# Two blocks of a mixed model, one core: the filter sums of the long convolution on GpSimd in place of VectorE

## The chip, the cores and the metric

One core of a Trainium2 chip runs the whole program once. The metric is device microseconds (us) of that core, as the median over several executions; each profile is one execution, recorded by the hardware profiler. Engines: PE is TensorE (PEld its weight loads), DVE is VectorE, ACT is ScalarE, POOL is GpSimd, and SP issues the DMAs.

## The reference, cut to what matters

A first block of two layers (pooling and attention, then a long convolution and a Fourier mixer) is followed by a second block of two layers. All is float32, 512 tokens, width 1024. The change concerns the filters of the long convolution only:

```python
h = (hdn @ w3).reshape(L, 2, 2, 768)                 # 2 orders, 2 directions, 768 channels
h = h * decay[:, None, None, :]
h = h / (jnp.sum(jnp.abs(h), axis=(0, 2), keepdims=True) + EPS)
kfull = jnp.concatenate([h[:, :, 0], zero, h[:0:-1, :, 1]], axis=0)
...
zf, kf = jnp.fft.rfft(z, n=2 * L, axis=1), jnp.fft.rfft(kfull, n=2 * L, axis=0)
return jnp.fft.irfft(zf * kf[None], n=2 * L, axis=1)[:, :L]
```

## The kernel before, in words

The program is five streams of instructions, one for each engine, written out by hand. Every instruction adds to a semaphore under a label, and `wait_ge(*when(label))` makes an engine wait for that label. An engine works strictly in the order of its stream. So the order of the work around the change is the order of these lines, and whatever stands behind a wait on an engine waits too.

The long convolution treats 768 channels in two halves of 384 (`G = 384`) and two orders, which makes four filters, n = 0 to 3 (`STEPS`). A filter has 512 lags, in four tiles j = 0 to 3 of 128 lags (partitions) by 384 channels. For a tile:

- TensorE (`filters`, L1610) multiplies the hidden layer with `W3`, one product for each direction, into PSUM.
- ScalarE (`decay`, L566) computes the decay `DEC`.
- VectorE (`filter_tile`, L1071) multiplies PSUM with `DEC` into `HH[0]` and `HH[1]`, the two directions. There is one buffer of each.
- VectorE forms `FSUM` (L1076) and `FDIFF` (L1077), their sum and difference, from which the spectrum's cosine and sine parts are made. In tile 0 it copies one row (L1081).
- ScalarE (`magnitudes`, L574) writes the magnitudes `MAG`, and VectorE adds them into `ABSA` (L1085, L1088 in tile 0).

After a filter's last tile TensorE adds `ABSA` over partitions (`norm_sums`, L1615), VectorE turns the result into the norm's inverse (`filter_norm`, L1095 and L1097), and TensorE transforms `FSUM` and `FDIFF` (`transform("hk", ...)`, L1627), after which VectorE combines even and odd parts (`spectrum`, L1109 to L1113).

Filter 0 is made in between the 18 tiles of a three-tap convolution: VectorE does two products with additions for each (L1161 and L1164, both of whose tensors lie in SBUF) and a one-column copy (L1163), and after tiles 2, 6, 10 and 14 (`FILTER_AT`) it does a filter tile. The filters n+1 = 1 to 3 are made in the loop over the steps n = 0 to 2. There VectorE's order is:

```python
filter_tile(n + 1, 0)
filter_tile(n + 1, 1)
spectrum("hz", n, 0)
filter_tile(n + 1, 2)
filter_tile(n + 1, 3)
filter_norm(n + 1)
products(n, 0)
```

and TensorE's order is `to_tokens(n)`, `filters` 0 and 1, `transform("hz", n, 0)`, `filters` 2 and 3, `norm_sums(n + 1)`, `transform("hz", n, 1)`, two `transform("hk", n + 1, ...)` and `back(n)` (L1647). `products` (L1128 to L1137) multiplies the spectra; `output` (L1146 to L1155) follows `back`.

GpSimd's stream before the change has the pooling mixer early in the program (L828 to L847), and then only clears a few tensors at the start of each layer of the second block (L852 to L855). VectorE's work beside the pooling mixer is the norm and rotation of the heads: L982 and L987 with both tensors in SBUF, L993 and L998 likewise, L995 with one of its operands in PSUM.

Of the kernel before, what the change touches and what calls it, by code (L numbers as in the profile page):

```python
# [56 lines left out]
class Ledger:  # L57
# [15 lines left out]
    def did(self, label, by=1):  # L73
        name = label.split(".")[0]
        if self.engine and name not in self.counts:
            name = f"{name.split('_')[0]}_on_{self.engine}"
        self.counts[name] = self.counts.get(name, 0) + by
        assert label not in self.marks, label
        self.marks[label] = (name, self.counts[name], tuple(k for k, _, _ in self.stack))
        return self.sem(name), by  # L80
# [6 lines left out]
    def when(self, label, back=None):  # L87
        if self.known is None:
            return self.sem("unknown_yet"), 1
        name, value, loops = self.known[0][label]  # L90
        for loop in loops:
            per = self.known[1][loop, name]
            here = [var for k, var, _ in self.stack if k == loop]
            if here:
                value = here[0] * per + (value - (per if back == loop else 0))
            else:
                value = value + (self.known[2][loop] - 1) * per
        return self.sem(name), value
# [19 lines left out]
def program(nc, A, known=None):  # L118
# [3 lines left out]
    add, sub, mul = ALU.add, ALU.subtract, ALU.mult  # L122
# [3 lines left out]
    did, when, sem = led.did, led.when, led.sem  # L126
# [5 lines left out]
    def at(offset, shape, dt=f32, name="t"):  # L132
        made[0] += 1
        return nc.alloc_sbuf_tensor_at(f"{name}_{made[0]}", shape, dt, offset=base + offset)
# [44 lines left out]
    def bank(b, n=S, rows=slice(0, P)):  # L179
        return PS[rows, b * S:b * S + n]  # L180

    def z(n, rows=slice(0, P)):
        return Z[rows, n * S:(n + 1) * S]
# [32 lines left out]
    G = 384  # L216
# [3 lines left out]
    FSUM = at(MOD_AT + 12 * KB, [P, 4, G], name="filter_sum")  # L220
    FDIFF = at(RAW_AT + 8 * KB, [P, 4, G], name="filter_diff")
# [3 lines left out]
    MAG = at(SPLIT_AT + 4 * KB, [P, 2, G], name="filter_mag")  # L225
# [10 lines left out]
    HH = [at(o, [P, G], name="filter") for o in (MOD_AT + 18 * KB, RAW_AT + 14 * KB)]  # L236
    PMY = [at(WIDE_AT + 24 * KB + 2 * KB * c, [P, S], name="hy_y") for c in range(2)]
    ABSA, DEC = SQ[0], SQ[1]
# [67 lines left out]
    STEPS = [(g, o) for g in range(2) for o in range(2)]  # L306
    FILTER_AT = (2, 6, 10, 14)
    SPEC_BANK = {"hk": 0, "hz": 4}
    ITEMS = [(h, i, br) for h in range(4) for i in range(NT) for br in range(3)]
    WIDTH = [31 if br == 2 else P * (i + 1) for _, i, br in ITEMS]  # L310
    GROUP_BANK = (0, 2, 5, 1)
    ROT_BANKS = (6, 1, 6, 1)
# [507 lines left out]
    @block.gpsimd  # L820
    def _(pool):
        led.engine = "gpsimd"
        gp = nc.gpsimd

        pool.wait_ge(taken, EV_IN + PRIME)
        pool.wait_ge(*when("in_tabc.all"))
        for c, t in enumerate((PU, PV_, PW_)):
            gp.memset(t[:, :, :], 0.0).then_inc(*did(f"pool_z.{c}"))  # L828
        pool.wait_ge(*when("pool_z.2"))
        for m in range(2):  # L830
            gp.tensor_copy(PU[:, m, 8:8 + S], z(10 + m)).then_inc(*did(f"pool_u.{m}"))
        pool.wait_ge(*when("pool_u.1"))
        gp.tensor_tensor(PV_[:, :, 0:527], PU[:, :, 0:527], PU[:, :, 1:528], add).then_inc(*did("pool_s.2"))
        pool.wait_ge(*when("pool_s.2"))
        gp.tensor_tensor(PW_[:, :, 0:525], PV_[:, :, 0:525], PV_[:, :, 2:527], add).then_inc(*did("pool_s.4"))
        pool.wait_ge(*when("pool_s.4"))
        gp.tensor_tensor(PV_[:, 1, 0:521], PW_[:, 1, 0:521], PW_[:, 1, 4:525], add).then_inc(*did("pool_s.8"))
        pool.wait_ge(*when("pool_s.8"))
        gp.tensor_tensor(PW_[64:P, 1, 0:513], PV_[64:P, 1, 0:513], PV_[64:P, 1, 8:521], add).then_inc(*did("pool_s.16"))
        pool.wait_ge(*when("pool_s.16"))  # L840
        for g, (w, src) in enumerate(((2, PV_), (4, PW_), (8, PV_), (16, PW_))):
            m, rows = g // 2, slice(64 * (g % 2), 64 * (g % 2) + 64)
            gp.tensor_tensor(Z[rows, (10 + m) * S:(11 + m) * S], src[rows, m, 8 - w // 2:8 - w // 2 + S], INVC[rows, m * S:(m + 1) * S], mul).then_inc(*did(f"pool_m.{g}"))
        for g in range(4):
            m, rows = g // 2, slice(64 * (g % 2), 64 * (g % 2) + 64)
            pool.wait_ge(*when(f"pool_m.{g}"))
            gp.tensor_tensor(Z[rows, (10 + m) * S:(11 + m) * S], Z[rows, (10 + m) * S:(11 + m) * S], PU[rows, m, 8:8 + S], sub).then_inc(*did("pool_d.all" if g == 3 else f"pool_d.{g}"))  # L847
        with led.loop(pool, "layers", LAYERS) as lay:
            pool.wait_ge(taken, lay * PER_LAYER + (T_LAYERS + L_OUT + PRIME))
            pool.sem_inc(passed, 1)  # L850
            for c in range(2):
                gp.memset(K2[c][:, :, :], 0.0).then_inc(*did(f"k_zero.{c}"))  # L852
            gp.memset(KC[:, :, :], 0.0).then_inc(*did("k_zero.all"))
            gp.memset(GS[:, :, :], 0.0).then_inc(*did("gla_zero.0"))
            gp.memset(GA[:, :, :], 0.0).then_inc(*did("gla_zero.1"))  # L855
# [3 lines left out]
    def _(dve):  # L859
        led.engine = "vector"  # L860
        v = nc.vector
# [201 lines left out]
        def filter_tile(n, j):  # L1063

            for d in range(2):
                dve.wait_ge(*when(f"hy_filt.{n}.{2 * j + d}"))
                if d == 0:
                    dve.wait_ge(*when(f"hy_dec.{n}.{j}"))
                if j or n:
                    dve.wait_ge(*when(f"hy_abs.{n if j else n - 1}.{(j - 1) % 4}.1"))  # L1070
                v.tensor_tensor(HH[d][:, :], bank(2 * (j % 2) + d, G), DEC[:, 0:G], mul).then_inc(*did(f"hy_d{d}.{n}.{j}"))  # L1071
            dve.wait_ge(*when(f"hy_d1.{n}.{j}"))
            if n:
                dve.wait_ge(*when(f"hk_mm.{n - 1}.1"))
                dve.wait_ge(*when(f"hy_norm_mm.{n - 1}"))
            v.tensor_tensor(FSUM[:, j, :], HH[0][:, :], HH[1][:, :], add).then_inc(*did(f"hy_sd.{n}.{j}.0"))  # L1076
            v.tensor_tensor(FDIFF[:, j, :], HH[0][:, :], HH[1][:, :], sub).then_inc(*did(f"hy_sd.{n}.{j}.1"))  # L1077
            if j == 0:

                dve.wait_ge(*when(f"hy_sd.{n}.{j}.0"))  # L1080
                v.tensor_copy(FSUM[0:1, 0, :], HH[0][0:1, :]).then_inc(*did(f"hy_lag0.{n}"))  # L1081
            for d in range(2):
                dve.wait_ge(*when(f"hy_mag.{n}.{j}.{d}"))
                if j:
                    v.tensor_tensor(ABSA[:, 0:G], ABSA[:, 0:G], MAG[:, d, :], add).then_inc(*did(f"hy_abs.{n}.{j}.{d}"))  # L1085
                    dve.wait_ge(*when(f"hy_abs.{n}.{j}.{d}"))
            if j == 0:
                v.tensor_tensor(ABSA[:, 0:G], MAG[:, 0, :], MAG[:, 1, :], add).then_inc(*did(f"hy_abs.{n}.{j}.1"))  # L1088

        def filter_norm(n):  # L1090
            inv = HINV[n % 2]
# [66 lines left out]
        for j in range(18):  # L1158
            dve.wait_ge(*when(f"conv_mid.{j}"))
            tap = TAP[j % 3]  # L1160
            v.scalar_tensor_tensor(tap[:, 1:S], z(j + 1)[:, 0:S - 1], col("conv_w", j), tap[:, 1:S], mul, add).then_inc(*did(f"conv1.{j}"))  # L1161
            dve.wait_ge(*when(f"conv1.{j}"))
            v.tensor_copy(z(j)[:, S - 1:S], tap[:, S - 1:S]).then_inc(*did(f"conv2.{j}"))  # L1163
            v.scalar_tensor_tensor(z(j)[:, 0:S - 1], z(j + 1)[:, 1:S], col("conv_w", 36 + j), tap[:, 0:S - 1], mul, add).then_inc(*did(f"conv3.{j}"))  # L1164
            if j in FILTER_AT:
                filter_tile(0, FILTER_AT.index(j))
# [3 lines left out]
        for n in range(len(STEPS)):  # L1170
            more = n + 1 < len(STEPS)
            if more:
# [3 lines that stand above are left out]
            if more:  # L1176
# [4 lines that stand above are left out]
            spectrum("hz", n, 1)  # L1181
            if more:
                spectrum("hk", n + 1, 0)
            products(n, 1)
            if more:
                spectrum("hk", n + 1, 1)
            for c in range(3):
                output(n, c)
# [875 lines left out]
```

## Time and profile before

| what | value |
|---|---|
| median of 3 runs | 2574.24 us |
| lowest and highest of these | 2568.61 and 2581.93 us |
| span of the profiled execution (the page gives no other time of it) | 2575.7 us |
| TensorE, VectorE, ScalarE, GpSimd busy | 2227.7, 1236.4, 882.5, 32.5 us |
| mean granted TensorE clock, as a share of full speed | 0.913 |

Busy time is that of an engine's own instructions; two engines may be busy at once. In rows of a timeline the first number is the start in us from the span's start, the second the time in us from the first instruction's start to the last one's end, and x is the number of instructions; an arrow in brackets names what ended the idle time before them. VectorE starts an instruction before the last one's end is recorded, so that starts lie closer than durations.

### The profile page before, as it was taken

How to read it: one execution, taken by the hardware profiler on the slowest of the kernel's cores; microseconds unless marked ns; L12 is line 12 of the kernel's file. 1: busy time of each engine (PE TensorE's matmuls, PEld its weight loads, DVE VectorE, ACT ScalarE, POOL GpSimd, SP SyncE). 2: the span in 40 equal slices, each digit the busy share in tenths (PEclk: the TensorE clock that was granted, in tenths of full speed). 3: DMA queues.
4: the chain of work that ended last, by engine and by line, in shares of the span. 5: the costliest groups of instructions: out<-in, count | busy, mean ns of one | idle time of the engine just before them, and what ended most of it. 6: DMA issues, size and time to landing. Idle time of an engine off the chain costs nothing.

```text
span 2575.7 us, 27482 instructions
## 1 busy us (share of the span) xinstructions
PE 2227.7 (86%) x9280; PEld 1649.3 (64%) x9280; DVE 1236.4 (48%) x2113; ACT 882.5 (34%) x1431; POOL 32.5 (1%) x31
## 2 busy tenths in 40 slices
PE   7797888996677978988877999997997877999996
PEld 5683446874345556855555788775865545878875
DVE  4656555566677663257425423324246634422423
ACT  2334433224211134234535323324224454322322
POOL 0003000000000000000000000000000000000000
PEclk8898999997799999977788999998987978999998
DMA  7362015772000151200011222222210010222222
GB/s 272 138 254 98 1 65 189 268 254 101 3 3 28 67 213 66 98 33 1 1 59 49 91 96 98 82 88 92 98 65 1 1 33 33 98 98 97 93 73 79
DMA packets 45850, 230.28 MB, mean 89 GB/s; under 512 B 4839, under 2 KB 6375, under 8 KB 28744
## 3 DMA queue, kind: packets, MB, share of 16 engines
q1 hardware_dynamic: 45768, 229.27, 24.7%
q8 instruction: 41, 0.67, 0.1%
q14 instruction: 41, 0.34, 0.0%
HBM read 227.16 MB, written 2.10 MB: 89 GB/s over the span
## 4 chain that ended last, share of the span: by engine, by line
PE 71%; DVE 15%; ACT 6%; issue 5%; DMA 3%; DVEq 0%; ACTq 0%; SPq 0%
PE banks L1453 16%; PE banks L1454 16%; PE banks L1455 16%; PE banks L1627 3%; PE banks L1474 2%; DMA mod_raw<-in_wmod 2%; DVE mod_acc L880 2%; PE banks L1647 2%; PE banks L1804 2%; PE banks L1568 1%; PE banks L1463 1%; PE banks L1483 1%; DVE h_low L900 1%; PE banks L1727 1%; DVE z L897 1%
## 5 line engine op out<-in xcount | busy, mean ns | idle before, releaser
L1453 PE MATMUL banks<-h_high,w_high 128*128 128x512 f32 x1504 | 609.1, 405 | 55.6 <-DVE h_low L900 31.5
L865 DVE TENSOR_TENSOR w_low<-w_raw,w_high 128x1024 fp32r<-128x1024 f32 x253 | 309.3, 1223 | 604.4 <-ACT w_high L415 603.6
L1454 PE MATMUL banks<-h_low,w_high 128*128 128x512 f32 x1504 | 595.3, 396 | 0.0
L1455 PE MATMUL banks<-h_high,w_low 128*128 128x512 f32 x1504 | 594.9, 396 | 0.0
L1453 PEld LDWEIGHTS banks<-h_high,w_high 128*128 128x128 f32 x1504 | 287.9, 191 | 139.7 <-issue 38.3
L415 ACT ACTIVATE w_high<-w_raw 128x1024 fp32r<-128x1024 f32 x253 | 266.2, 1053 | 212.7 <-PE banks L1455 178.4
L1454 PEld LDWEIGHTS banks<-h_low,w_high 128*128 128x128 f32 x1504 | 289.2, 192 | 61.2 <-issue 4.4
L1455 PEld LDWEIGHTS banks<-h_high,w_low 128*128 128x128 f32 x1504 | 288.2, 192 | 61.7
L1453 PE MATMUL banks<-hidden_high,w_high 128*128 128x512 f32 x512 | 211.0, 412 | 6.2 <-DVE hidden_low L1422 6.2
L1454 PE MATMUL banks<-hidden_low,w_high 128*128 128x512 f32 x512 | 202.5, 395 | 0.0
L1455 PE MATMUL banks<-hidden_high,w_low 128*128 128x512 f32 x512 | 202.2, 395 | 0.0
L420 ACT ACTIVATE z<-banks 128x512 f32 (+1 forms) x92 | 55.0, 598 | 358.6 <-PE banks L1455 358.6
L880 DVE SCALAR_TENSOR_TENSOR mod_acc<-mod_raw,silu_cond,mod_acc 128x1024 f32<-128x1024 f32 x112 | 143.7, 1283 | 11.7 <-DVE mod_acc L880 1.2
L1420 DVE CAST hidden_high<-sq 128x512 f32 x64 | 27.3, 427 | 195.7 <-ACT sq L808 195.7
L1453 PEld LDWEIGHTS banks<-hidden_high,w_high 128*128 128x128 f32 x512 | 98.3, 192 | 32.0 <-issue 11.9
L1454 PEld LDWEIGHTS banks<-hidden_low,w_high 128*128 128x128 f32 x512 | 98.3, 192 | 25.1 <-issue 4.9
L1455 PEld LDWEIGHTS banks<-hidden_high,w_low 128*128 128x128 f32 x512 | 98.0, 191 | 20.9
L806 ACT ACTIVATE relu<-banks 128x512 f32<-128x512 f32 x64 | 38.3, 598 | 205.0 <-PE banks L1455 205.0
L1474 PE MATMUL banks<-sq,eye 128*128 128x512 f32 (+1 forms) x128 | 70.2, 703 | 28.3 <-ACT sq L430 28.3
L1474 PEld LDWEIGHTS banks<-sq,eye 128*128 128x128 f32 x128 | 25.4, 230 | 71.2 <-ACT sq L430 64.7
L1788 PE MATMUL banks<-probs_t,v_tok 128*128 128x128 f32 x320 | 57.8, 320 | 5.9 <-ACT probs_t L716 5.2
L1804 PE MATMUL banks<-k_rope,q_rope 128*128 128x128 f32 (+3 forms) x128 | 61.4, 570 | 0.0
(359 smaller groups left out, 2613.2 us busy)
## 6 DMA issues: line engine op xcount, KB each, us to landing
w_raw<-in_wt SPq DMA_DIRECT2D x129, 1024.0 KB, 4.8
mod_raw<-in_wmod SPq DMA_DIRECT2D x144, 512.0 KB, 4.9
cmp_w<-in_cmp_w SPq DMA_DIRECT2D x2, 2048.0 KB, 8.2
x<-in_xT SPq DMA_DIRECT2D x1, 2048.0 KB, 9.7
dft<-in_dft SPq DMA_DIRECT2D x1, 2048.0 KB, 10.3
out_x<-x SPq DMA_DIRECT2D x1, 2048.0 KB, 7.1
tab_attn<-in_tab_attn SPq DMA_DIRECT2D x1, 1216.0 KB, 7.5
ctx_in<-in_ctxT SPq DMA_DIRECT2D x1, 1024.0 KB, 12.0
```

The lines of the kernel that those rows point to most:

```text
L415: nc.scalar.activation(WH[b % 2][:, :, :].rearrange("p k c -> p (k c)"), RAW[b // 2][:, b % 2, :], ACT.Copy).then_inc(w_high, 1)
L420: nc.scalar.activation(dst, bank(b), func).then_inc(taken, 1)
L865: v.tensor_tensor(WL[b % 2][:, :, :].rearrange("p k c -> p (k c)"), RAW[b // 2][:, b % 2, :], WH[b % 2][:, :, :].rearrange("p k c -> p (k ...
L880: v.scalar_tensor_tensor(ACC[:, :], MOD[k % 4][:, :], c, ACC[:, :], mul, add).then_inc(mod_used, 1)
L1453: mm(out, WH[b % 2][:, k, :], H[:, kk, :], start=start and k == 0, stop=False)
L1454: mm(out, WH[b % 2][:, k, :], L[:, kk, :], start=False, stop=False)
L1455: last = mm(out, WL[b % 2][:, k, :], H[:, kk, :], start=False, stop=stop and k == KT - 1)
L1474: mm(bank(b, n), ONES, SQ[k % 2][:, 0:n], start=k == 0, stop=k == KT - 1).then_inc(*did(f"{tag}_ss.{k}"))
L1627: last = mm(bank(SPEC_BANK[kind] + 2 * c + e, G), FWD[:, e, c, t, ft * P:(ft + 1) * P], rhs, start=t == 0, stop=t == 1)
L1647: last = mm(bank(4 + c)[:, e * 256:(e + 1) * 256], GSP[:, ft, 2 * s_ + e, c * P:(c + 1) * P], INV[:, e, s_, ft, :], start=k == 0, stop=k == 3)
L1788: last = mm(out, [VS_, VW_][br][:, j, :], PT2[n % 2][:, j, :], start=br == 0 and j == 0, stop=False)
L1804: mm(bank(SCORE_BANKS[n % 4], WIDTH[n]), QR[:, h // 2, i * P:(i + 1) * P], K2[br][:, h % 2, 0:WIDTH[n]], start=True, stop=True).then_inc(* ...
```

## The change

The sum, the difference, the one-row copy and the additions of the magnitudes leave VectorE's stream and become a function `filter_sums(n, j)` in GpSimd's, which stands behind the pooling mixer and runs over n = 0 to 3 and j = 0 to 3. VectorE keeps the two products of each tile; before it overwrites `HH` it now waits for the previous tile's difference (GpSimd) and magnitudes (ScalarE), in place of the previous tile's last magnitude addition. The copy of a row in tile 0 stands ahead of the difference. ScalarE, TensorE and SP have the same lines as before; where they wait for an addition, it is now one of GpSimd's.

```diff
+        def filter_sums(n, j):
+            pool.wait_ge(*when(f"hy_d1.{n}.{j}"))
+            if n and j == 0:
+                pool.wait_ge(*when(f"hk_mm.{n - 1}.1"))
+                pool.wait_ge(*when(f"hy_norm_mm.{n - 1}"))
+            gp.tensor_tensor(FSUM[:, j, :], HH[0][:, :], HH[1][:, :], add).then_inc(*did(f"hy_sd.{n}.{j}.0"))
+            if j == 0:
+                pool.wait_ge(*when(f"hy_sd.{n}.{j}.0"))
+                gp.tensor_copy(FSUM[0:1, 0, :], HH[0][0:1, :]).then_inc(*did(f"hy_lag0.{n}"))
+            gp.tensor_tensor(FDIFF[:, j, :], HH[0][:, :], HH[1][:, :], sub).then_inc(*did(f"hy_sd.{n}.{j}.1"))
+            for d in range(2):
+                pool.wait_ge(*when(f"hy_mag.{n}.{j}.{d}"))
+                if j:
+                    gp.tensor_tensor(ABSA[:, 0:G], ABSA[:, 0:G], MAG[:, d, :], add).then_inc(*did(f"hy_abs.{n}.{j}.{d}"))
+                    pool.wait_ge(*when(f"hy_abs.{n}.{j}.{d}"))
+            if j == 0:
+                gp.tensor_tensor(ABSA[:, 0:G], MAG[:, 0, :], MAG[:, 1, :], add).then_inc(*did(f"hy_abs.{n}.{j}.1"))
+
+        for n in range(len(STEPS)):
+            for j in range(4):
+                filter_sums(n, j)
...
                 if j or n:
-                    dve.wait_ge(*when(f"hy_abs.{n if j else n - 1}.{(j - 1) % 4}.1"))
+                    prev = f"{n if j else n - 1}.{(j - 1) % 4}"
+                    dve.wait_ge(*when(f"hy_sd.{prev}.1"))
+                    dve.wait_ge(*when(f"hy_mag.{prev}.1"))
                 v.tensor_tensor(HH[d][:, :], bank(2 * (j % 2) + d, G), DEC[:, 0:G], mul).then_inc(*did(f"hy_d{d}.{n}.{j}"))
-            dve.wait_ge(*when(f"hy_d1.{n}.{j}"))
-            if n:
-                dve.wait_ge(*when(f"hk_mm.{n - 1}.1"))
-                dve.wait_ge(*when(f"hy_norm_mm.{n - 1}"))
-            v.tensor_tensor(FSUM[:, j, :], HH[0][:, :], HH[1][:, :], add).then_inc(*did(f"hy_sd.{n}.{j}.0"))
-            v.tensor_tensor(FDIFF[:, j, :], HH[0][:, :], HH[1][:, :], sub).then_inc(*did(f"hy_sd.{n}.{j}.1"))
-            if j == 0:
-
-                dve.wait_ge(*when(f"hy_sd.{n}.{j}.0"))
-                v.tensor_copy(FSUM[0:1, 0, :], HH[0][0:1, :]).then_inc(*did(f"hy_lag0.{n}"))
-            for d in range(2):
-                dve.wait_ge(*when(f"hy_mag.{n}.{j}.{d}"))
-                if j:
-                    v.tensor_tensor(ABSA[:, 0:G], ABSA[:, 0:G], MAG[:, d, :], add).then_inc(*did(f"hy_abs.{n}.{j}.{d}"))
-                    dve.wait_ge(*when(f"hy_abs.{n}.{j}.{d}"))
-            if j == 0:
-                v.tensor_tensor(ABSA[:, 0:G], MAG[:, 0, :], MAG[:, 1, :], add).then_inc(*did(f"hy_abs.{n}.{j}.1"))
```

## Rows read from the trace of the kernel before

**Rows 1.** The page, busy us of each engine (share of the span), instructions.

```profile
PE 2227.7 (86%) x9280; PEld 1649.3 (64%) x9280; DVE 1236.4 (48%) x2113; ACT 882.5 (34%) x1431; POOL 32.5 (1%) x31
```

**Rows 2.** The page, the chain that ended last, share of the span by engine.

```profile
PE 71%; DVE 15%; ACT 6%; issue 5%; DMA 3%; DVEq 0%; ACTq 0%; SPq 0%
```

**Rows 3.** Busy time by stage: stretch, length, PE, PEld, DVE, ACT, POOL, clock, DMA.

```profile
617.60:657.30 39.70, 11.59 (x22) 5.90 (x22) 38.62 (x80) 19.73 (x31) 0.00 (x0) 0.54 0.02 5
...
677.00:730.50 53.50, 40.25 (x135) 26.19 (x135) 41.07 (x71) 9.32 (x20) 0.00 (x0) 0.94 0.02 4
```

**Rows 4.** Timeline of the first stage, filter tiles 0 and 3.

```profile
623.27 0.56 DVE L1076 TENSOR_TENSOR filter_sum<-filter,filter 128x384 f32<-128x384 f32 x1
...
624.95 0.73 DVE L1161 SCALAR_TENSOR_TENSOR conv_taps<-z,cols,conv_taps 128x511 f32<-128x511 f32 x1
...
650.44 0.56 DVE L1076 TENSOR_TENSOR filter_sum<-filter,filter 128x384 f32<-128x384 f32 x1
...
652.57 0.75 DVE L1161 SCALAR_TENSOR_TENSOR conv_taps<-z,cols,conv_taps 128x511 f32<-128x511 f32 x1
...
652.59 1.44 PE L1615 MATMUL banks<-eye,sq 128*128 128x1 f32 x6 [17.62 <-DVE sq L1085]
...
657.10 0.15 DVE L1095 TENSOR_SCALAR norm_gain<-banks 128x3 f32<-128x3 f32 x1
```

**Rows 5.** Timeline of step 0, VectorE, ScalarE and TensorE.

```profile
677.96 1.20 DVE L1071 TENSOR_TENSOR filter<-banks,sq 128x384 f32<-128x384 f32 x2 [1.07 <-PE banks L1610]
...
687.51 1.01 DVE L1071 TENSOR_TENSOR filter<-banks,sq 128x384 f32<-128x384 f32 x2
...
691.37 0.99 ACT L574 ACTIVATE filter_mag<-filter 128x384 f32<-128x384 f32 x2 [1.78 <-DVE filter L1071]
...
692.78 1.14 DVE L1085 TENSOR_TENSOR sq<-sq,filter_mag 128x384 f32<-128x384 f32 x2
...
693.98 1.44 PE L1615 MATMUL banks<-eye,sq 128*128 128x1 f32 x6 [6.39 <-DVE sq L1085]
...
695.53 0.16 DVE L1095 TENSOR_SCALAR norm_gain<-banks 128x3 f32<-128x3 f32 x1 [1.61 <-PE banks L1615]
```

**Rows 6.** The chain that ended last: start us, us, what.

```profile
693.98 1.44 PE banks L1615 x6
695.42 12.19 PE banks L1627 x32
...
806.20 1.44 PE banks L1615 x6
```

**Rows 7.** GpSimd's groups by line and shape: busy us, mean ns.

```profile
L847 POOL TENSOR_TENSOR z<-z,pool 64x512 f32<-64x512 f32 x4 | 5.1, 1266 | 0.3
...
L833 POOL TENSOR_TENSOR pool<-pool 128x1054 f32<-128x1054 f32 x1 | 1.9, 1942 | 0.1
...
L831 POOL COPY pool<-z 128x512 f32<-128x512 f32 x2 | 1.2, 612 | 0.1
L837 POOL TENSOR_TENSOR pool<-pool 128x521 f32<-128x521 f32 x1 | 1.1, 1119 | 0.1
...
232.70 5.29 POOL L847 TENSOR_TENSOR z<-z,pool 64x512 f32<-64x512 f32 x4
```

**Rows 8.** VectorE's groups by line, 225 to 230.4 us, GpSimd busy beside it.

```profile
L987 DVE SCALAR_TENSOR_TENSOR zn<-z,cols,rs_s 128x512 f32<-128x512 f32 x2 | 3.2, 1661 | 0.0
L993 DVE TENSOR_TENSOR rope_a<-zn,tab_attn 128x512 f32<-128x512 f32 x1 | 1.6, 1580 | 0.0
...
L995 DVE TENSOR_TENSOR rope_b<-banks,tab_attn 128x512 f32<-128x512 f32 x1 | 0.7, 677 | 0.0
```

**Rows 9.** VectorE's groups by line, 240 to 262 us, GpSimd idle.

```profile
L993 DVE TENSOR_TENSOR rope_a<-zn,tab_attn 128x512 f32<-128x512 f32 x7 | 4.8, 684 | 0.0
...
L987 DVE SCALAR_TENSOR_TENSOR zn<-z,cols,rs_s 128x512 f32<-128x512 f32 x6 | 4.5, 745 | 9.0 <-ACT rs_s L515 9.0
```

**Rows 10.** As rows 3, the first 3 us from the norm sums on.

```profile
694.00:697.00 3.00, 3.00 (x9) 2.39 (x10) 1.43 (x4) 0.00 (x0) 0.00 (x0) 0.50 0.00 0
```

## The prediction

> **What bounds the kernel now.** I first read the shares of busy time. TensorE leads with 86% and GpSimd has 1% [rows 1], so GpSimd has room. But a share is a mean over stages, so I then read the chain that ended last: 71% of it is TensorE, 15% VectorE and nothing is GpSimd [rows 2]. The 16 filter tiles touched here run from 622 to 806 us, so I read that part by stage [rows 3].
>
> *Stage A*, 617.6 to 657.3 us, is the short convolution with the first four filter tiles (n=0) between its taps. VectorE is busy for 38.6 of 39.7 us and TensorE for 11.6: VectorE alone bounds it, and each us off its queue could shorten the stage.
>
> *Stage B* is the three loop steps (n=0, 1, 2) that also make the filters of n+1. No engine fills it: VectorE has 41.1 of 53.5 us [rows 3]. What ends last is read from the two queues. In step 0 VectorE makes tiles 2 and 3 from 687.51 us, the last magnitude addition (L1085) ends at 692.78+1.14=693.92, and at 693.98 TensorE starts the norm sums (L1615), after idling [rows 5]. TensorE works in order, so 32 matmuls (12.2 us) stand behind them, and VectorE waits for the sums' result at L1095, with the spectrum products behind it [rows 5, 6]. The chain has this link in all three steps, of which the first and the last stand in the rows [rows 6]. So in stage B the latency from tile 2's products to tile 3's last magnitude addition counts, not VectorE's load.
>
> **The change, part by part.**
>
> *What leaves VectorE.* In the first tile of a filter, sum, difference, one-row copy and one addition take from 623.27 to 624.95, 1.68 us; in each of the others, sum, difference and two additions take from 650.44 to 652.57, 2.13 us [rows 4]. (Four filters have four tiles each.) In stage A that is 1.68+3x2.13=8.1 us, the most that it could gain.
>
> *What GpSimd takes.* The trace has no 384-element tensor_tensor on GpSimd, so I bound it. Two operands of different tensors and 512 elements: 1.266 us, while VectorE is idle. Operands from one tensor: 1.942 us at 1054 elements and 1.119 at 521 [rows 7]. The latter two give 1.54 ns per element over a fixed 0.315 us, so 0.91 us at 384. The 512 row over the same fixed part gives 1.86 ns per element, so 0.315+0.71=1.03. The 60 moved additions and subtractions read two tensors or two far parts of one, as the 512 row does, so I take 1.02 and keep 0.91 and 1.10 as ends. Between two of them 0.07 us pass: four of L847 spanned 5.29 us, (5.29-1.27)/3=1.34 apart [rows 7]. So one each 1.09 us. The copy of 384 elements in one partition is under the 0.61 us of a 512-element copy [rows 7]; I take 0.5. A tile is thus 4x1.09=4.4 us on GpSimd, the first of a filter 3x1.09+0.57=3.8.
>
> The Trainium skill (GPSIMD Engine Reference, section 3.1) measures a two-input add of 2048 elements at 4497 ns; an estimate by proportion from that page is 0.84 us plus a share of fixed cost, inside the same bounds.
>
> *Stage B.* Tile 2's products end at 687.51+1.01=688.52 [rows 5]. GpSimd is free: tile 0's work starts at 677.96+1.20=679.2 [rows 5] and takes till 683.0; tile 1's products now wait for tile 0's difference (681.9), so they end at 682.9, and GpSimd is done with tile 1 at 687.4. That delay of tile 1 is covered by TensorE's transform; VectorE's next spectrum, which waits for that transform, comes before 687.51 either way. From 688.52 GpSimd has tiles 2 and 3 in one unbroken run: eight instructions, 8x1.09-0.07=8.65 us, plus 0.06 for the hand-over, ends at 697.23. Tile 3's products now wait for tile 2's difference (690.7) and end at 691.8, before GpSimd comes to them at 692.9, so that wait costs nothing. The magnitudes of tile 3 on ScalarE wait for tile 2's last addition (692.9) and take 1 us [rows 5], while GpSimd does the sum and difference: nothing either. TensorE's norm sums start at 697.3 instead of 693.98: **+3.3 us**. Everything behind them, TensorE's 32 matmuls and VectorE's products, hangs on them and has no slack of its own to give. Three steps: **+9.9 us**. With 0.91 us an instruction it is +2.4 a step (7.3), with 1.10 +4.0 (11.9).
>
> TensorE idles that much longer. Its granted clock is 0.50 in the 3 us from the sums on [rows 10], the 1.2 GHz level, after a pause of 6.4 us [rows 5]. That a pause of 10 us costs more is not excluded: 0 to 1 us a step. I take 0, since the six matmuls of the sums take 1.44 us after 6.4 us of pause [rows 5] as after 17.6 us [rows 4].
>
> *Stage A.* GpSimd's 15 additions and subtractions and one copy now lie beside VectorE's convolution taps, each of which reads two tensors in SBUF. The trace shows what that does: beside GpSimd, L987 took 1.66 us on average and L993 1.58 [rows 8], without it 0.745 and 0.684 [rows 9]; L995, with one operand in PSUM, took only 0.68 [rows 8]. So one 512-element GpSimd instruction delays VectorE by about 0.9 us, while it itself takes 1.27 alone. At 384 elements I scale that to 0.9x0.75=0.67, and take off 0.1, because the taps of one tile (L1161, copy, L1164) wait for each other's ends and so leave a small gap in which GpSimd can read: 0.57. Four per tile are 2.3 us, against 2.13 removed: +0.2 for each of three tiles. The first has three and a copy, 3x0.57+0.2=1.9, against 1.68: +0.2. Tile 3 needs more care, since L1095 (657.10) waits for the norm sums, which are hidden today: they ended at 652.59+1.44=654.03 [rows 4]. VectorE reaches L1095 at 650.44+2.3+4.53 (three tap tiles, 652.57 to 657.10)=657.3. GpSimd, taking turns, needs its 0.71 us of data and one tap's 0.55 between, some 1.25 us an instruction, so it ends near 650.5+5.1=655.6, and the sums at 657.1: just covered. Stage A: **+0.8, rounded to +1 us**. Bounds: without interference VectorE gains 1.68+2x2.13=5.9 on three tiles, and on the last the sums end at 650.5+4.3+1.5=656.3 instead of 657.10, so -6.7; the upper bound is the second rival's.
>
> The new waits on GpSimd's queue block nobody else: its next other work comes after 1100 us. No DMA is moved; none is issued by GpSimd.
>
> *Sum.* +9.9+1=+11 us on a span of 2575.7 us. The page gives no other time for this execution; its span stands 1.5 us above the median of the three runs, 2574.24. I apply the difference to the median: **2585 us**, +0.43%.
>
> **The rivals.**
>
> *No interference in stage A.* If the taps mostly pass by, A gives -6.7 and B +9.9: +3, 2577 us. Against it stand the rows of L987 and L993 [rows 8]; for it, that the taps have gaps.
>
> *Slower: the lock holds for the whole instruction.* If each GpSimd instruction shuts VectorE's taps out for its full 1.02 us, tiles 1 to 3 cost 4x1.02-2.13=+1.95 each and tile 0 3x1.02+0.5-1.68=+1.9, so A is +7.7, with B +17.6: 2592 us, +0.68%. It decides once the delay per instruction is above about 0.7 us. For it: L987 went from 0.745 to 1.66 on average [rows 8, 9], 0.92 of GpSimd's 1.27. Against it: that is 72%, not all.
> The Trainium skill (SBUF — State Buffer, section "Who interferes with whom") says the second comer is blocked until the first finishes its whole instruction, for two SBUF inputs against a GpSimd read; by that rule this case would hold. The trace agrees on who is hit, less so on how long.
>
> *Faster.* If GpSimd did 384 elements in VectorE's 0.57 us (half of L1085's 1.14 [rows 5]) and did not disturb, its eight instructions would take 4.9 us from 688.52, where VectorE now takes 5.4 to 693.92: -0.5 a step. With -8 for stage A that is 2565 us, and beyond 0.5% only with the spread of runs. All rows of GpSimd speak against it.
>
> **How the numbers follow.** My forecast, with its own spread of GpSimd's price, has 0.57, no interference 0.15, the full lock 0.23, the fast GpSimd 0.05. A measurement of this kernel can tell about 0.5%, 12.9 us, from no change: slower begins at 2587. The forecast's upper part (1.10 us an instruction, or a clock that costs 1 us a step) reaches over that with 0.14, so slower has 0.37. Of the fast GpSimd's 0.05 I give faster 0.03; same has 0.60. The range takes in no interference (2577, and two us of spread in runs) and the full lock: 2575 to 2593.
>
> **What would show it.** The norm sums should start 3 us later in each of the three steps, with GpSimd's L1085-like additions as their releaser and about 1.0 us each; VectorE should idle some 7 us before the norm's L1095. Taps in stage A should take up to 1.3 us each where GpSimd runs, and the stage should end within 2 us of where it does now. If the stage is 6 us shorter, the interference was overrated; if GpSimd's instructions take 0.8 us or less, stage B is nearly even and the forecast is too high.

## The result: 1.0048 of the time before, and the profile after

| | before | after |
|---|---|---|
| median, 9 runs each | 2581.93 us | 2592.37 us |
| lowest and highest | 2568.61, 2588.42 | 2584.97, 2602.16 |
| ratio, 95% interval | | 1.0048 [1.0025, 1.007] |
| span of the profiled execution | 2575.7 us | 2589.5 us |

The change costs 0.48%, by the medians 10.4 us. The interval excludes no change; the 0.5% at which the prediction let a slower kernel begin lies inside it. (The first three runs of before, with 2574.24 as their median, had been on its fast side. That the 2592.37 us equal the 2592 of the prediction's rival of the full lock is owed to this: its ratio was 1.0068.)

The page of the changed kernel, busy time of each engine and the chain that ended last:

```profile
PE 2218.7 (86%) x9280; PEld 1646.4 (64%) x9280; DVE 1211.8 (47%) x2049; ACT 882.3 (34%) x1431; POOL 95.1 (4%) x95
...
PE 71%; DVE 14%; ACT 6%; issue 5%; DMA 2%; POOL 1%; DVEq 0%; ACTq 0%; SPq 0%
```

VectorE is 24.6 us less busy, GpSimd 62.6 us more [rows 1], and GpSimd is now on the chain with 1% [rows 2]. The busy time by stage shows where (stretch, length, then PE, PEld, DVE, ACT, POOL, the clock): stage A from the first tap to L1102, which is L1095 of before; then the two transforms of filter 0; then the three loop steps.

```profile
618.01:662.07 44.06, 11.56 (x22) 5.86 (x22) 38.26 (x63) 19.64 (x30) 17.42 (x16) 0.58 0.02 5
662.07:681.35 19.28, 15.28 (x44) 9.01 (x45) 4.23 (x11) 3.49 (x9) 0.00 (x0) 0.84 0.00 0
681.35:737.52 56.17, 40.28 (x134) 26.24 (x135) 33.16 (x55) 9.18 (x20) 15.09 (x16) 0.91 0.01 4
737.52:796.18 58.66, 41.91 (x146) 27.71 (x146) 35.31 (x58) 10.98 (x24) 15.08 (x16) 0.91 0.02 4
796.18:853.80 57.62, 41.59 (x147) 27.56 (x147) 33.09 (x55) 10.98 (x24) 15.08 (x16) 0.91 0.15 50
```

The same five stretches of before:

```profile
617.69:657.10 39.41, 11.50 (x22) 5.81 (x22) 38.45 (x79) 19.64 (x30) 0.00 (x0) 0.54 0.02 5
657.10:677.03 19.93, 15.93 (x44) 9.24 (x45) 4.23 (x11) 3.49 (x9) 0.00 (x0) 0.81 0.00 0
677.03:730.49 53.46, 40.24 (x134) 26.15 (x135) 41.07 (x71) 9.29 (x20) 0.00 (x0) 0.94 0.02 4
730.49:786.07 55.58, 41.54 (x147) 27.50 (x147) 43.09 (x74) 11.09 (x24) 0.00 (x0) 0.94 0.02 4
786.07:842.99 56.92, 43.60 (x147) 28.47 (x147) 41.16 (x71) 11.14 (x24) 0.00 (x0) 0.91 0.15 51
```

Stage A is 4.65 us longer. In it VectorE is as busy as before, with 16 instructions fewer: what was moved away came back as longer ones. The steps are 2.71, 3.08 and 0.70 us longer, and the stretch between is 0.65 shorter, with a clock of 0.84 for 0.81. Together +10.5 us. At 906 us of before, a first shared point behind all of it, the two traces are 10.2 us apart, of which 0.3 had arisen ahead of stage A. In stages that the change doesn't touch the distance then goes down to 5.2 us (at 1137 us of before) and up to the spans' 13.8: two executions differ by some us in such stages. So the stretches of the trace carry the argument, not the spans.

*Stage A, one tile.* The timeline of the changed kernel around filter tile 1 (start, us, engine):

```profile
632.92 1.01 DVE L1095 TENSOR_TENSOR filter<-banks,sq 128x384 f32<-128x384 f32 x2
633.51 0.99 ACT L574 ACTIVATE filter_mag<-filter 128x384 f32<-128x384 f32 x2 [3.67 <-DVE filter L1095]
...
634.01 1.00 POOL L854 TENSOR_TENSOR filter_sum<-filter,filter 128x384 f32<-128x384 f32 x1 [6.93 <-DVE filter L1095]
634.40 2.21 ACT L595 ACTIVATE conv_taps<-z,cols 128x512 f32<-128x512 f32 x3
634.97 1.00 POOL L858 TENSOR_TENSOR filter_diff<-filter,filter 128x384 f32<-128x384 f32 x1
635.23 1.29 DVE L1168 SCALAR_TENSOR_TENSOR conv_taps<-z,cols,conv_taps 128x511 f32<-128x511 f32 x1 [1.29 <-ACT conv_taps L595]
635.92 2.85 POOL L862 TENSOR_TENSOR sq<-sq,filter_mag 128x384 f32<-128x384 f32 x2
...
636.62 1.30 DVE L1171 SCALAR_TENSOR_TENSOR z<-z,cols,conv_taps 128x511 f32<-128x511 f32 x1
637.84 1.48 DVE L1168 SCALAR_TENSOR_TENSOR conv_taps<-z,cols,conv_taps 128x511 f32<-128x511 f32 x1
```

Two things are seen. VectorE first idles for 1.29 us, because ScalarE writes the next middle tap (L595, from 634.40) only after the magnitudes (L574). Before, sum, difference and additions lay over that wait, and VectorE was still busy with the last of them (632.96+1.14=634.10) when the tap, begun at 632.44, was ready:

```profile
632.44 2.21 ACT L595 ACTIVATE conv_taps<-z,cols 128x512 f32<-128x512 f32 x3
...
632.96 1.14 DVE L1085 TENSOR_TENSOR sq<-sq,filter_mag 128x384 f32<-128x384 f32 x2
...
634.14 0.75 DVE L1161 SCALAR_TENSOR_TENSOR conv_taps<-z,cols,conv_taps 128x511 f32<-128x511 f32 x1
```

And three taps of the changed kernel take 1.29, 1.30 and 1.48 us for 0.74, together +1.84: the interference. The ends show what a tap waits for. Of the two additions that the timeline above joins, the first is

```profile
635.92 1.45 POOL L862 TENSOR_TENSOR sq<-sq,filter_mag 128x384 f32<-128x384 f32 x1
```

So GpSimd's difference ends at 635.97, its additions at 637.37 and 638.77, and the three taps end at 636.52, 637.92 and 639.32, each 0.55 us later. A tap that starts while GpSimd's instruction is running gets no further until that instruction has ended; it loses what was left of it, and not its whole length. GpSimd waits for VectorE in the same way: its additions end 0.85 us after the tap before them and take 1.45 and 1.32 us for 1.0. The 0.55 us hold for every tap of stage A that was held up, counted from the last GpSimd instruction that it waited for; the one tap that waited for more than one is taken up further down.

The groups of stage A add it up; first after, then before:

```profile
L1168 DVE SCALAR_TENSOR_TENSOR conv_taps<-z,cols,conv_taps 128x511 f32<-128x511 f32 x18 | 19.4, 1078 | 8.6 <-ACT conv_taps L595 8.6
L1171 DVE SCALAR_TENSOR_TENSOR z<-z,cols,conv_taps 128x511 f32<-128x511 f32 x18 | 15.0, 834 | 0.0
```

```profile
L1161 DVE SCALAR_TENSOR_TENSOR conv_taps<-z,cols,conv_taps 128x511 f32<-128x511 f32 x18 | 13.4, 746 | 3.5 <-ACT conv_taps L595 3.3
L1164 DVE SCALAR_TENSOR_TENSOR z<-z,cols,conv_taps 128x511 f32<-128x511 f32 x18 | 13.4, 742 | 0.0
```

Interference 34.4-26.8=7.6 us, waiting for ScalarE 8.6-3.5=5.1 us (the 3.5 lie ahead of the stage's first tap in both), less the 8.1 us removed [rows 4]: +4.6.

*A loop step.* The timeline of step 0 of the changed kernel, to be read beside [rows 5]:

```profile
692.92 0.99 POOL L854 TENSOR_TENSOR filter_sum<-filter,filter 128x384 f32<-128x384 f32 x1 [1.50 <-DVE filter L1095]
...
693.87 0.99 POOL L858 TENSOR_TENSOR filter_diff<-filter,filter 128x384 f32<-128x384 f32 x1
694.82 2.06 POOL L862 TENSOR_TENSOR sq<-sq,filter_mag 128x384 f32<-128x384 f32 x2
695.06 1.02 DVE L1095 TENSOR_TENSOR filter<-banks,sq 128x384 f32<-128x384 f32 x2 [2.29 <-POOL filter_diff L858]
...
698.86 2.06 POOL L862 TENSOR_TENSOR sq<-sq,filter_mag 128x384 f32<-128x384 f32 x2
700.98 1.44 PE L1622 MATMUL banks<-eye,sq 128*128 128x1 f32 x6 [9.06 <-POOL sq L862]
...
702.46 0.16 DVE L1102 TENSOR_SCALAR norm_gain<-banks 128x3 f32<-128x3 f32 x1 [6.37 <-PE banks L1622]
```

GpSimd's eight instructions run unbroken from 692.92 to 700.92, 8.0 us. The norm sums start 700.98-681.35=19.63 us after the step's first filter matmul (L1617), and 19.62 and 19.61 in the next two steps, against 693.98-677.03=16.95, then 16.90 and 18.58 before. (In the 18.58 eight filter matmuls took 4.42 us; in the two other steps they took 2.8.) VectorE then idles 6.37 us in front of L1102, and in this step everything behind follows from the norm sums at the same distance as before: `back` 23.56 us after them, for 23.52.

### The profile page after: what moved, and what is told of

It is laid out like the page before. It is cut to its first block, busy times and chain, and to the rows that moved or that the text cites. A ratio compares the mean times of both kernels' runs of the same rounds, so it can differ in the third digit from the quotient of the medians.

```text
span 2589.5 us, 27491 instructions
## 1 busy us (share of the span) xinstructions
PE 2218.7 (86%) x9280; PEld 1646.4 (64%) x9280; DVE 1211.8 (47%) x2049; ACT 882.3 (34%) x1431; POOL 95.1 (4%) x95
## 4 chain that ended last, share of the span: by engine, by line
PE 71%; DVE 14%; ACT 6%; issue 5%; DMA 2%; POOL 1%; DVEq 0%; ACTq 0%; SPq 0%
PE banks L1460 16%; PE banks L1461 16%; PE banks L1462 16%; PE banks L1634 3%; PE banks L1481 2%; DVE mod_acc L902 2%; DMA mod_raw<-in_wmod 2%; PE banks L1654 2%; PE banks L1811 1%; PE banks L1575 1%; PE banks L1470 1%; PE banks L1795 1%; PE banks L1490 1%; DVE h_low L922 1%; DVE z L919 1%
## 5 line engine op out<-in xcount | busy, mean ns | idle before, releaser
L728 ACT ACTIVATE probs<-banks,stats 128x31 f32<-128x31 f32 (+4 forms) x72 | 32.2, 447 | 90.1 <-DVE stats L1357 86.7
```

## The experiments

Theory 1: two separate losses. In stage A the moved work comes back as interference and as ScalarE's latency laid bare; in a loop step GpSimd's serial chain delays the norm sums, behind which TensorE's queue keeps 32 matmuls.

### One half at a time

Filter 0 alone on GpSimd (e1), and filters 1 to 3 alone (e2, with `range(1, len(STEPS))` in the line below); the others are VectorE's, as before (the lines that give them back to it are left out here).

```diff
-        for n in range(len(STEPS)):
+        for n in (0,):
             for j in range(4):
                 filter_sums(n, j)
```

> Only filter 0's sums (stage A, between the convolution taps) are GpSimd's; filters 1 to 3 are VectorE's as before. Theory 1 (two separate losses: stage A pays interference and ScalarE's late taps, stage B pays GpSimd's serial chain): from the first tap (L1168) to the norm's L1102 some 44.0 us, as in the changed kernel (44.06), against 39.41 before; in each of the three loop steps the norm sums start some 16.9 us after the step's first filter matmuls, as before. Span about +4.6 us. Rival (stage A's loss is a state of the execution, or the stages are coupled): stage A under 41 us.

> Only filters 1 to 3 (the loop) are GpSimd's; filter 0 is VectorE's as before. Theory 1: stage A 39.4 us as before; in each step the norm sums start 2.7 us later counted from the step's first filter matmuls. Span +8 us, less what the clock gives back. Rival (the shift of each step comes from GpSimd having been left late by the step before): first step under 1.5 us later.

Stage A of e1, from 619.52 to L1123, the line of the norm:

```profile
619.52 0.75 DVE L1189 SCALAR_TENSOR_TENSOR conv_taps<-z,cols,conv_taps 128x511 f32<-128x511 f32 x1 [3.68 <-ACT conv_taps L595]
...
663.58 0.15 DVE L1123 TENSOR_SCALAR norm_gain<-banks 128x3 f32<-128x3 f32 x1
```

That is 44.06 us, to the hundredth that of the changed kernel. Its norm sums come 16.95, 17.58 and 17.15 us into the steps; in the step of the 17.58 the first eight filter matmuls took 3.42 us for 2.8. In e2 stage A is 39.40 us, and the first step reads:

```profile
679.15 2.82 PE L1638 MATMUL banks<-hy_w,hdn 128*128 128x384 f32 x8 [1.23 <-DVE k_spec L1141]
...
698.77 1.44 PE L1643 MATMUL banks<-eye,sq 128*128 128x1 f32 x6 [9.06 <-POOL sq L862]
```

19.62 us again. The two losses are separate and each as large as in the changed kernel. The whole times, one execution each, don't show it (2592.73 and 2589.8 us beside 2577.61 before): terms of 5 and 8 us are within the spread of runs, and only the stretches of the trace tell them apart.

### The wait for ScalarE

In the changed kernel, ScalarE writes the next middle tap ahead of the magnitudes.

```diff
             if j in FILTER_AT:
                 decay(0, FILTER_AT.index(j))
-                magnitudes(0, FILTER_AT.index(j))
+            if j - 1 in FILTER_AT:
+                magnitudes(0, FILTER_AT.index(j - 1))
```

> The changed kernel, but ScalarE writes the next tile's middle tap before the filter tile's magnitudes. Theory 1 (VectorE's 1.29 us of waiting for ScalarE's tap after each filter tile is an exposed latency that the moved sums used to cover): the four waits are gone, and one more tap instruction per tile falls beside GpSimd, which costs some 0.6 us; stage A is 4x0.7 = 2.8 us shorter than in the changed kernel, about 41.3 us. Rival (the interference alone counts and the wait only lies beside it): stage A stays within 0.5 us of 44.06.

Stage A took 41.55 us (620.20 to 661.75), 2.5 less than in the changed kernel. Its groups:

```profile
L1169 DVE SCALAR_TENSOR_TENSOR conv_taps<-z,cols,conv_taps 128x511 f32<-128x511 f32 x18 | 19.9, 1107 | 3.5 <-ACT conv_taps L595 3.5
L1172 DVE SCALAR_TENSOR_TENSOR z<-z,cols,conv_taps 128x511 f32<-128x511 f32 x18 | 17.2, 957 | 0.0
```

The wait is back at its 3.5 us, and the taps take 37.1 us for 34.4: interference is now 10.3 us, 2.6 a tile. So the wait was a real loss, and half of it had stood in for interference. Even so the stage is 2.1 us longer than before: the 8.1 us removed don't pay for the interference. The gain shows in stage A alone: the one execution took 2593.38 us, and its loop steps were longer than the changed kernel's, at granted clocks of 0.88, 0.89 and 0.86 for 0.91.

### What interferes

In stage A GpSimd writes a constant (e4, the diff below), or copies one operand (e5, `gp.tensor_copy(FSUM[:, j, :], HH[0][:, :])`), in place of each addition and subtraction. Filter 0's sums, differences and magnitude sums are left out in both; of the four edited lines one is shown.

```diff
-            gp.tensor_tensor(FSUM[:, j, :], HH[0][:, :], HH[1][:, :], add).then_inc(*did(f"hy_sd.{n}.{j}.0"))
+            (gp.tensor_tensor(FSUM[:, j, :], HH[0][:, :], HH[1][:, :], add) if n else gp.memset(FSUM[:, j, :], 1.0)).then_inc(*did(f"hy_sd.{n}.{j}.0"))
```

> In stage A GpSimd writes a constant (memset) in place of each sum, difference and magnitude addition: filter 0's arithmetic is left out. Theory 1 (a tap is held up only while GpSimd reads SBUF): every tap instruction takes 0.74 us as without GpSimd, and stage A loses 1.84 us per tile against the changed kernel (2.05 on the first, where the row copy still reads): some 36.6 us. Rival (any GpSimd instruction holds the taps up): two or three taps per tile take over 1.0 us.

> In stage A GpSimd copies one operand in place of each addition and subtraction: filter 0's arithmetic is left out. Theory 1 (reads hold the taps up, for as long as GpSimd reads): copies take about 0.5 us and read for 0.3 of it, so two or three taps per tile are stretched by up to 0.35 us each; stage A some 38 us. Rival (only a second GpSimd operand collides): taps at 0.74 us throughout, as with the constant.

Stage A took 36.43 us with the constants and 36.83 with the copies. The taps, constants first, then copies:

```profile
L1168 DVE SCALAR_TENSOR_TENSOR conv_taps<-z,cols,conv_taps 128x511 f32<-128x511 f32 x18 | 13.4, 747 | 8.6 <-ACT conv_taps L595 8.6
L1171 DVE SCALAR_TENSOR_TENSOR z<-z,cols,conv_taps 128x511 f32<-128x511 f32 x18 | 13.4, 742 | 0.0
```

```profile
L1168 DVE SCALAR_TENSOR_TENSOR conv_taps<-z,cols,conv_taps 128x511 f32<-128x511 f32 x18 | 13.6, 755 | 8.6 <-ACT conv_taps L595 8.6
```

Writes don't hold a tap up: theory 1's number (36.6) holds. With copies I was wrong by a us: the taps are stretched by a hundredth on average, and GpSimd gives way too, as its own groups in e5 show (L862, the copies that fall beside taps, 0.68 us for 0.51):

```profile
L862 POOL COPY sq<-filter_mag 128x384 f32<-128x384 f32 x6 | 4.1, 682 | 0.2
L854 POOL COPY filter_sum<-filter 128x384 f32<-128x384 f32 x4 | 2.0, 506 | 404.4 <-DVE filter L1095 404.4
```

The average hides that single taps were held up, for example the second one after tile 0:

```profile
626.59 1.00 POOL L865 COPY sq<-filter_mag 128x384 f32<-128x384 f32 x1
...
627.34 0.80 DVE L1171 SCALAR_TENSOR_TENSOR z<-z,cols,conv_taps 128x511 f32<-128x511 f32 x1
```

The copy ends at 627.59 and the tap 0.55 us later, as beside an addition. A tap alone takes 0.74 us, so it is stretched only if GpSimd's instruction ends more than 0.19 us after the tap's start, and few copies do. So a one-operand read holds a tap up as well, and the expectation's rival (only a second operand collides) falls; the copies were mostly too short to be felt. A constant shows no such effect: every tap beside one took 0.75 us.

### TensorE's queue

The norm sums go behind `transform("hz", n, 1)`, in the kernel before (e6) and in the changed one (e7).

```diff
                 filters(n + 1, 3)
-                norm_sums(n + 1)
             else:
                 over_channels()
             transform("hz", n, 1)
+            if more:
+                norm_sums(n + 1)
```

> The kernel before, but TensorE's norm sums stand behind transform hz 1 instead of ahead of it. Theory 1 (the norm sums gate a loop step only because TensorE's queue puts 32 matmuls behind them): 16 of the 32 matmuls run in the 6.4 us in which TensorE waits today, and k_spec's first instruction comes 3 us earlier per step, after which VectorE's products bind: -3 to -4 us a step, about -10 us. Rival (VectorE's products, 7.3 us, and the spectrum bind in any case): under -1 us a step.

> The changed kernel with the same move of the norm sums. Theory 1: the norm sums still end GpSimd's chain, so the step gains the same 3 to 4 us as e6 gives before, and e7 stays some 2.7 us a step plus stage A's 4.6 above e6: about 12 us above e6. Rival (with TensorE's queue free, GpSimd's latency is covered): e7 within 6 us of e6.

e6: 0.9965 [0.9944, 0.9985] of before, and in a second series, whose expectation stands further down, 0.9975 [0.9961, 0.9988]. e7: 1.0012 [0.9991, 1.0032]. It was expected 12 us above e6, and the rival said under 6. The medians are 7.9 us apart and the ratios 0.47%, 12 us; from the first tap to the end of the three steps the two profiles are 228.0-215.7=12.3 us apart. In their profiles the first two steps (from filter matmul to filter matmul) take 52.05 and 52.86 us in e6 (before 55.00 and 55.59), 53.84 and 56.30 in e7 (changed kernel 57.71 and 58.67). So taking the matmuls from behind the norm sums gains 2.95 and 2.73 us before and 3.87 and 2.37 after, but does not cover GpSimd: in e7 VectorE still waits

```profile
701.63 0.16 DVE L1102 TENSOR_SCALAR norm_gain<-banks 128x3 f32<-128x3 f32 x1 [5.78 <-PE banks L1622]
```

### Only what nobody waits for

Filter 0 on VectorE. For filters 1 to 3 GpSimd makes sum and difference alone, VectorE the magnitude additions, and the products alternate between two pairs of buffers.

```diff
+    HHS = [HH, [RS[:, 0:G], Z[:, 18 * S:18 * S + G]]]
...
+        def filter_sums(n, j):
+            H2 = HHS[j % 2]
+            pool.wait_ge(*when(f"hy_d1.{n}.{j}"))
...
+            gp.tensor_tensor(FSUM[:, j, :], H2[0][:, :], H2[1][:, :], add).then_inc(*did(f"hy_sd.{n}.{j}.0"))
...
+            gp.tensor_tensor(FDIFF[:, j, :], H2[0][:, :], H2[1][:, :], sub).then_inc(*did(f"hy_sd.{n}.{j}.1"))
```

> Filter 0 as before. For filters 1 to 3 GpSimd makes only sum and difference, which nothing waits for until the transform; VectorE keeps the magnitude additions, and the products go to two sets of buffers. Theory 1 (in the loop the chain product, magnitude, addition, norm sums counts, and the sum and difference do not): the two tiles ahead of the norm sums take 2x2.3 us instead of 6.4, so the norm sums start 1.8 us earlier per step: some -5 us, below both kernels. Rival (a wait for GpSimd or ScalarE takes the place): norm sums no earlier than before.

It missed: 1.0041 [1.0023, 1.0058], and the norm sums came 18.11 us into step 0 instead of 15.1. VectorE's groups from 688 to 697 us:

```profile
L1104 DVE TENSOR_TENSOR sq<-sq,filter_mag 128x384 f32<-128x384 f32 x4 | 5.2, 1299 | 0.3
L1091 DVE TENSOR_TENSOR filter<-banks,sq 128x384 f32<-128x384 f32 x2 | 1.0, 548 | 0.0
```

The four magnitude additions, now beside GpSimd's sums, take 1.30 us for 0.56, while the products out of PSUM (L1091) keep their 0.55. It looks like the interference of stage A on another pair of instructions: each of the four ends 0.41 to 0.42 us after GpSimd's instruction. To test that, GpSimd writes constants for sum, difference and copied row of filters 1 to 3, and that arithmetic is left out:

```diff
-            gp.tensor_tensor(FSUM[:, j, :], H2[0][:, :], H2[1][:, :], add).then_inc(*did(f"hy_sd.{n}.{j}.0"))
+            gp.memset(FSUM[:, j, :], 1.0).then_inc(*did(f"hy_sd.{n}.{j}.0"))
```

> The split kernel (sum and difference on GpSimd, magnitude additions on VectorE, two sets of buffers, filters 1 to 3), with GpSimd writing a constant in place of sum, difference and copied row of filters 1 to 3: that arithmetic is left out. Theory 1 (the split kernel lost because VectorE's magnitude additions, with both operands in SBUF, are held up by GpSimd's reads: 1.31 us each instead of 0.56): the additions take 0.56 us again and the norm sums start 14.5 to 15.5 us after the step's first filter matmul, against 18.1 in the split kernel and 16.95 before. Rival (the loss is in waits for ScalarE's magnitudes or decay): still 17 us or more.

```profile
L1104 DVE TENSOR_TENSOR sq<-sq,filter_mag 128x384 f32<-128x384 f32 x4 | 2.2, 558 | 0.3
```

(VectorE's groups from 692.9 to 698.3 us.) The norm sums came 15.16, 15.43 and 15.10 us into the steps. So the plan of the split kernel was right as to when the norm sums start, and it was GpSimd's reads that delayed them. The gain behind them was smaller than that: from the first tap to the end of the three steps e10 took 222.0 us for 225.3 before, 3.3 less where e8's expectation had 5. In step 0 nothing was left of it: between norm sums and `back` the granted clock was 0.80 for 0.90, and that stretch took 24.28 us for 23.52. The one execution took 2579.52 us, within the runs of before.

### A version without GpSimd

e6 and VectorE's norm between its second and third spectrum product:

```diff
             for m, (a, b_) in enumerate(((0, 0), (2, 2), (0, 2), (2, 0))):
+                if m == 2 and ft == 0 and n + 1 < len(STEPS):
+                    filter_norm(n + 1)
...
                 filter_tile(n + 1, 3)
-                filter_norm(n + 1)
             products(n, 0)
```

> No work on GpSimd. The kernel before with the norm sums behind transform hz 1 (as e6) and, new, VectorE's norm between the second and the third spectrum product, so that it does not idle for the 1.6 us of the norm sums. Theory 1 (once TensorE's queue is free, VectorE's products bind the step): 1.4 to 1.6 us a step below e6, about -4.5 us, so some 11 to 14 us below before, ratio near 0.995. Rival (the transform hk 0 becomes late instead): no faster than e6's 0.9965.

> The same kernel as e6_norm_later_before, on the chip of e11, so that the two are compared: theory 1 gives e11 about 4.5 us less than this, the rival no difference.

e11 has 0.9976 [0.9962, 0.9991], e6 again 0.9975 [0.9961, 0.9988]: no gain over e6 is seen, but the 4.5 us expected are only 0.17%, and each interval reaches 0.14% to either side. In step 0 what the rival said happened, transform hk 0 became late:

```profile
710.40 0.56 DVE L1109 TENSOR_TENSOR k_spec<-banks,k_odd 128x384 f32<-128x384 f32 x1 [1.45 <-ACT k_odd L588]
```

VectorE waits 1.45 us here for what it saved earlier. That transform's first eight matmuls took 5.49 us in this step, against 4.54 in both profiles of e6. In the next two steps the wait was 0 and 0.06 us, and VectorE reached the same instruction 9.4 and 9.6 us after the norm sums, for 10.4 in e6. So the rival is seen in one step of three, and why the whole time shows nothing of the other two stays open. e6, the simpler edit, beats both kernels, by 0.25 to 0.35% of before.

## Why the prediction had the sum nearly right and the outcome wrong

The forecast was +11 us, 2585 us by the three runs then at hand; measured are +10.4 us by the medians, and 10.2 us between the traces at 906 us. Yet it named no change as likeliest (0.60, slower 0.37), and the kernel is slower, clear of no change. Two steps failed. The step of the mechanism is stage A: it took VectorE's next taps as ready, forecast +1 us, and the runs showed +4.65. The step of the outcome is "a measurement of this kernel can tell about 0.5%": nine runs told 0.48% to within 0.23%, so its own sum of +0.43% spoke for slower. Point by point:

- *Stage B gates at the norm sums, and all three steps shift whole:* right, as far as nothing else moved. Forecast +3.3 us a step, measured +2.7 for the norm sums in the first two steps; in the third, where before had slow filter matmuls, +1.0. The term that was off is the spacing of GpSimd's instructions. Its price, 1.02 us, was measured at 0.99 to 1.00. But between two with nothing to wait for no 0.07 us pass; the next starts 0.04 before the end, so they are 0.95 apart. The eight took 8.0 us, not 8.65.
- *Stage A +1 us:* wrong, +4.65. The step that failed is the one that took VectorE's next taps as ready. "VectorE reaches L1095 at 650.44+2.3+4.53" has no wait in it, and the prediction named ScalarE's part of stage A nowhere. I had asked who waits for GpSimd, not what the removed work had covered. The row was in the trace: ScalarE's next taps (L595) start after the magnitudes. It costs 1.29 us a tile, 5.1 in all.
- *Interference:* right in kind and nearly in size. Forecast 2.3 us a tile, and 1.9 for the first; measured 1.84 to 1.89 and 2.05, where the first GpSimd instruction fell into the wait, and 2.6 once that wait was taken away (e3).
- *The clock costs nothing:* it gave a little back. The stretch behind stage A was 0.65 us shorter, and step 2 grew by only 0.70, because its eight filter matmuls took 2.75 us for 4.42. In the steps that is 6.5 us instead of 3x2.7=8.1. This is no effect of the change that could be counted on: in the two profiles of e6's one kernel the first eight matmuls of transform hk 0 in step 1 took 2.85 and 4.54 us. The forecast's 10.9 plus stage A's 3.65, less 1.8 for the spacing, 0.65 and 1.6 for the clock, is the 10.5 us of the five stretches: the close sum is luck, an error of 3.65 us against three of 4.05 together.
- *The rival of the full lock* gave +7.7 for stage A; e3, the kernel in which all four instructions of a tile meet taps, has +2.1. Its price fell, but not its mechanism. It charged each GpSimd instruction at its full 1.02 us; a tap waits to the end of one that is already running, and by then part of it has passed. The prediction's own argument against it, "that is 72%, not all", misread rows of this kind, as the trace of before shows:

```profile
226.34 2.92 POOL L843 TENSOR_TENSOR z<-pool,tab_attn 64x512 f32<-64x512 f32 x2
...
228.22 1.58 DVE L993 TENSOR_TENSOR rope_a<-zn,tab_attn 128x512 f32<-128x512 f32 x1
```

  GpSimd's instruction ends at 229.26 and VectorE's at 229.80, 0.54 us later, as the taps did.

  The Trainium skill (SBUF — State Buffer, section "Who interferes with whom") has the right pairs: two SBUF inputs on VectorE against GpSimd's reads, not its writes, and no effect on an operand from PSUM. All three are borne out by e4, e8 and e10. That the second comer is blocked for the whole instruction of the first agrees with the ends above; what it pays is the rest of that instruction, 0.55 to 0.74 us beside one of 1.0. One case doesn't fit: the first tap after tile 0 took 2.79 us for 0.74 and ended 0.55 us after the third GpSimd instruction, not after the one that ran when it started.

```profile
624.69 0.49 POOL L857 COPY filter_sum<-filter 1x384 f32<-1x384 f32 x1
624.85 2.79 DVE L1168 SCALAR_TENSOR_TENSOR conv_taps<-z,cols,conv_taps 128x511 f32<-128x511 f32 x1 [1.29 <-ACT conv_taps L595]
...
626.10 0.98 POOL L865 TENSOR_TENSOR sq<-filter_mag 128x384 f32<-128x384 f32 x1
```

  The same happened in e1, e3 and e7, and in e8 to one magnitude addition in each step (2.59 us for 0.56), always during GpSimd's one-row copy or the difference behind it. Why VectorE was not let in between them stays open.
- *No interference* gave -6.7 for stage A; the kernel with constants has -3.0, for the wait for ScalarE is then all that is left.
- *The fast GpSimd* needed 0.57 us an instruction; each took 1.0.

## What to carry to other kernels

Before work is moved off an engine, look at what stands behind it in that engine's queue and whether its inputs would be ready that much earlier: here 5.1 of 8.1 us only uncovered a wait for ScalarE. Two-input work in SBUF on GpSimd is no free second VectorE: in stage A it held VectorE's own two-input instructions up for 7.6 us and took 8.1 off it. Beside PSUM-fed work it cost VectorE nothing, but took 1.0 us for 0.55. To price such interference from a trace, compare ends and not only durations: here a held instruction ended a fixed time after GpSimd's. And where a wait gates a queue, first ask what can be put ahead of it: moving one line of TensorE's order gained 0.25 to 0.35%, more than any placing of the sums did.

## What the runs showed that I had not expected

- A 384-element constant written by GpSimd takes 0.41 us and holds nothing up. A copy takes 0.51 us and holds a tap up by 0.12 us at most; beside taps it is itself stretched (0.68 us). An addition of two SBUF tensors takes 1.0 us and stretches taps by 0.55 to 0.74 us and VectorE's additions by 0.74 on average.
- A VectorE instruction held up by GpSimd ends a fixed time after GpSimd's: 0.55 us with 511 or 512 elements, 0.41 to 0.42 us with 384 (e8).
- GpSimd starts an instruction that waits for nothing 0.04 us before the last one's end (693.87 after 692.92+0.99).
- With the middle taps ahead of the magnitudes GpSimd's sum and difference took 1.4 us each for 1.0: beside each other both engines lose.
